# Prompt's selected and window attention: both heads' weights scaled on GpSimd, none on VectorE

## The reference, cut to what matters

```python
s = jnp.where(mask[:, :, None, None, :], s, NEG)
m = jnp.max(s, axis=-1, keepdims=True)
p = jnp.exp(s - m)
l = jnp.sum(p, axis=-1, keepdims=True)
o = jnp.einsum('bqgrk,bkgd->bqgrd', (p / l).astype(v.dtype), v)
...
o_nsa = (gate[:, :, 0, :, :, None] * o_cmp + gate[:, :, 1, :, :, None] * o_sel
         + gate[:, :, 2, :, :, None] * o_win)
```

## Time and profile before

| | |
|---|---|
| median of 3 runs | 2716.4 us (2714.63 to 2722.9) |
| the profiled execution's own time | 2721.63 us |
| its span, first to last instruction | 2718.8 us |
| TensorE busy over the span | 2513.0 us, 92% |
| VectorE, ScalarE, GpSimd busy | 1172.3, 934.7, 853.3 us |
| the stage `nsa_prompt` | about 471 to 634 us |

### The profile page before, as it was taken

How to read it: one execution, slowest core, us unless ns; L and a number is a source line. 1 busy time by engine, 2 the same in 40 slices (tenths; PEclk the granted TensorE clock), 3 DMA queues, 4 the chain that set the end, 5 groups by cost and what they waited for, 6 DMA issues and landing times. The chain is left out here.

```text
span 2718.8 us, 44972 instructions
## 1 busy us (share of the span) xinstructions
PE 2513.0 (92%) x18691; PEld 2248.3 (83%) x18691; DVE 1172.3 (43%) x2554; ACT 934.7 (34%) x1769; POOL 853.3 (31%) x434
## 2 busy tenths in 40 slices
PE   8889999997999999999988998899988888999997
PEld 8856796555989999998987897787765688999997
DVE  6884403776223222242754464441146424322225
ACT  4442221564332121133453464322135434221121
POOL 2350330332254333334333333323310026433331
PEclk9999998998999999999999899889998998999999
DMA  5212375450222222222221121113320822222221
GB/s 179 80 45 87 64 146 158 157 215 4 63 63 78 94 78 78 94 78 88 75 69 34 34 78 37 33 63 101 95 95 1 233 82 70 83 89 78 82 89 51
DMA packets 206728, 232.78 MB, mean 86 GB/s; under 512 B 40508, under 2 KB 165276, under 8 KB 205918
## 3 DMA queue, kind: packets, MB, share of 16 engines
q1 hardware_dynamic: 204446, 229.66, 27.3%
q10 hardware_dynamic: 2080, 0.25, 0.1%
HBM read 207.93 MB, written 48.35 MB: 94 GB/s over the span
## 5 line engine op out<-in xcount | busy, mean ns | idle before, releaser
L295 POOL TENSOR_TENSOR WRr<-WR,WH 128x2048 fp32r<-128x2048 f32 (+2 forms) x100 | 441.2, 4412 | 962.4 <-ACT WH L283 948.5
L2428 PE MATMUL PS<-HHr,WRr 128*128 128x288 f32 x1104 | 326.6, 296 | 0.0
L535 PE MATMUL PS<-YTr,WRr 128*128 128x288 f32 x1024 | 303.6, 297 | 0.0
L283 ACT CAST WH<-WR 128x2048 fp32r<-128x2048 f32 (+2 forms) x100 | 182.3, 1823 | 343.9 <-DMA WR<-in_mlp_w 141.6
L535 PE MATMUL PS<-HHr,WH 128*128 128x288 f32 (+1 forms) x896 | 271.4, 303 | 12.2 <-PEq L114 6.7
L535 PE MATMUL PS<-YTr,lt_WX 128*128 128x288 f32 x1408 | 282.1, 295 | 0.0
L535 PE MATMUL PS<-HHr,WRr 128*128 128x288 f32 (+1 forms) x896 | 268.3, 299 | 0.0
L535 PE MATMUL PS<-HTr,WH 128*128 128x288 f32 (+1 forms) x896 | 268.3, 299 | 0.0
L295 POOL TENSOR_TENSOR WRr<-WR,lt_WX 128x2048 fp32r<-128x2048 f32 x34 | 157.9, 4644 | 254.6 <-ACT lt_WX L283 254.6
L2428 PE MATMUL PS<-HHr,WH 128*128 128x288 f32 x800 | 236.8, 296 | 0.3 <-POOL WRr L295 0.3
L2428 PE MATMUL PS<-HTr,WH 128*128 128x288 f32 x800 | 236.2, 295 | 0.0
(11 more groups left out here) (685 smaller groups left out, 5680.2 us busy)
## 6 DMA issues: line engine op xcount, KB each, us to landing
WR<-in_mlp_w SPq DMA_DIRECT2D x64, 1024.0 KB, 5.2
WR<-in_cd_w_in SPq DMA_DIRECT2D x34, 1024.0 KB, 5.2
out_dil_s<-in_cache_dil_kv SPq DMA_DIRECT2D x2, 7936.0 KB
WR<-in_ab_w_in SPq DMA_DIRECT2D x12, 1024.0 KB, 5.2
past_rows<-in_cache_nsa_kv SPq DMA_DIRECT2D x16, 256.0 KB, 3.4
WR<-in_ab_w_in SPq DMA_DIRECT2D x16, 256.0 KB, 4.4
WR<-in_nsa_ck_w SPq DMA_DIRECT2D x4, 1024.0 KB, 5.4
WR<-in_nsa_cv_w SPq DMA_DIRECT2D x4, 1024.0 KB, 5.7
```

The costliest lines, as they stand in the source:

```text
L283: act.copy(high_slot(K, i, used), K.WR[:, n % RING, 0:used]).then_inc(K.hi, 1)
L295: pool.tensor_tensor(K.WRr[:, n % RING, 0:used], K.WR[:, n % RING, 0:used], high_slot(K, i, used).bitcast(F32), ALU.subtract).then_inc(K.l ...
L535: last = pe.matmul(out, a, b, start=(n == 0), stop=(n == 3 * len(terms) - 1))
L2428: last = pe.matmul(out, a[:, k, c], h[:, k, x], start=(n == 0), stop=(n == 3 * KT - 1))
```

## The change

GpSimd now scales both heads of a unit, one operation after the other, and VectorE none. `back(u)` on VectorE keeps the reciprocal alone. The two semaphores `p_even` and `p_odd` become one, `p_ready`, which both GpSimd operations raise; TensorE and ScalarE wait for it once in place of twice.

```diff
@@ turn(u), TensorE
-                    pe.wait_ge(p_even, u + 1)
-                    pe.wait_ge(p_odd, u + 1)
+                    pe.wait_ge(p_ready, 2 * (u + 1))
@@ exponentials, ScalarE
-                        act.wait_ge(p_even, u - 2)
-                        act.wait_ge(p_odd, u - 2)
+                        act.wait_ge(p_ready, 2 * (u - 2))
@@ GpSimd
-                    pool.tensor_scalar(E[:, u % 3, 0, 0:L], E[:, u % 3, 0, 0:L], sm[:, u % 3, 0:1], gate(u, 0),
-                                       ALU.mult, ALU.mult).then_inc(p_even, 1)
+                    for g in range(2):
+                        pool.tensor_scalar(E[:, u % 3, g, 0:L], E[:, u % 3, g, 0:L], sm[:, u % 3, g:g + 1], gate(u, g),
+                                           ALU.mult, ALU.mult).then_inc(p_ready, 1)
@@ back(u), VectorE
                     dve.reciprocal(sm[:, u % 3, :], sm[:, u % 3, :]).then_inc(r_ready, 1)
-                    dve.wait_ge(r_ready, u + 1)
-                    L = (units[u][1] + 1) * P
-                    dve.tensor_scalar(E[:, u % 3, 1, 0:L], E[:, u % 3, 1, 0:L], sm[:, u % 3, 1:2], gate(u, 1),
-                                      ALU.mult, ALU.mult).then_inc(p_odd, 1)
```

More of the change, by code:

```diff
@@ L1948, in nsa_prompt @@
         sm = sb("p_sm", [P, 3, 2])
-        with stage(nc, "s_mm", "nm_ready", "exp_done", "r_ready", "p_even", "p_odd", "turned", "t_act", "t_dve", "pv_done",
-                   "y_out", "zeroed", "gates_out", "dve_link") as (block, s_mm, nm_ready, exp_done, r_ready, p_even, p_odd, turned, t_act, t_dve,
+        with stage(nc, "s_mm", "nm_ready", "exp_done", "r_ready", "p_ready", "turned", "t_act", "t_dve", "pv_done",
+                   "y_out", "zeroed", "gates_out", "dve_link") as (block, s_mm, nm_ready, exp_done, r_ready, p_ready, turned, t_act, t_dve,
                                             pv_done, y_out, zeroed, gates_out, dve_link):
```

## The result

The changed kernel takes 2725.7 us (median of 20 runs, 2717.4 and up) against 2718.1 for the kernel before beside it. The ratio is 1.0023, with the 95% interval [1.0015, 1.0030]: 6.3 us slower. By the forecast's own basis, 2716.4 us, the ratio makes 2722.6. Either way it is above the forecast 2713.3 and outside its range. It is less than 0.3%, so among the chances it falls under "no change that can be told", but sign and size of the reasoning were wrong.

What follows compares the result with a forecast made beforehand. TensorE's own stream was taken as most of the stage, so only its waits could go. Gains of 1.8 + 0.9 + 0.6 = 3.3 us, less 0.2, gave net -3.1: 2716.4 becomes 2713.3 us, range 2709 to 2721.

Steps and rivals of the forecast that it cites:

- no change that can be told: For the whole kernel, a result within 0.3%, 8 us, of the kernel before; chance 0.9.
- What comes after the barrier has the same work and starts earlier by that: Behind the prompt's stage, later stages were to do the same work and pass on the stage's net -3.1 us.
- The scaling's price on GpSimd: One GpSimd scaling alone was to take about 0.29, 0.40, 0.50, 0.61 us for the four lengths, a pair 0.53 to 1.17.
- the rival without an exclusion: VectorE and GpSimd do not exclude each other; each GpSimd scaling costs 0.52 to 1.04 us again: +7 us, 2723.5; chance 0.12.
- the first rival: GpSimd's fixed part per scaling is at its upper bound, 0.41 us: +1.0 to +1.6 us in all, 2718; chance 0.2.
- the point at which I had the sign turn: In the prompt's stage, gain was to become loss where GpSimd's pair of 512-column scalings costs about 1.5 us.
- the sign of a wrong forecast: A pair of 512 columns over 1.5 us, or turns 20 to 22 waiting for GpSimd, would make the forecast wrong.
- The merged semaphore: One wait for two was to take 0.11 us off every turn (a unit's transposes) that waits for ScalarE's copy.
- VectorE's relief: Without its scaling, VectorE's output copy was to start 0.14 us behind the reciprocal, not 0.53, 0.39 us gained at turn 27.
- The period: The prompt's stage repeats every eight units; this was to take 19.5 to 19.6 us rather than 20.0, all the gain there.
- the tail at the barrier: At the stage's end GpSimd might be 0.13 us later at the barrier after its last pair; 0.2 us allowed.

Runs made afterwards that it cites:

- e2: The kernel before, with TensorE waiting for VectorE's scaling by name only in unit 0 (63 wait instructions fewer); ratio 1.0016 to the kernel before.
- e3: The changed kernel once more, unedited, for a second profile; ratio 1.0041 to the kernel before.
- e7: The changed kernel with head 1's weights left unscaled, so GpSimd scales once per unit; the prompt's stage takes 159.68 us, 163.51 in the changed kernel.
- e9: The kernel before with 192 more wait instructions on TensorE's list, for things past, in `scores`; ratio 1.0040 to the kernel before.
- e5: The changed kernel with a second wait on its one semaphore before each turn, restoring TensorE's list to 16741 instructions; ratio 0.9999 to the kernel before.
- e13: The changed kernel with 60 padding waits in `scores` for what is long past, TensorE's list at 16737 instructions; ratio 0.9988 to the kernel before.
- e10: The kernel before with one more VectorE memset of 1024 numbers at the end of the prompt's stage; ratio 1.0016 to the kernel before.
- e1: The changed kernel with the two semaphores `p_even` and `p_odd` kept apart, TensorE's list as long as before; ratio 1.0022 to the kernel before.
- e15: e1 once more, unedited, for a second profile; one run, the prompt's stage takes 165.23 us.
- e14: The kernel before with only the order of waits in `turn` changed, the two copies first, the weights' semaphores last; ratio 0.9996 to the kernel before.
- e11: The changed kernel with padding waits in `scores`, of which those for ScalarE's copy were not past; ratio 1.0145 to the kernel before.

## Why the prediction was wrong

- **"What comes after the barrier has the same work and starts earlier by that"** is the step that failed. The work is the same; the list is not. In the five profiles whose list is cut at that place (changed, e2, e3, e7, e9) C is 75.00 to 80.65, mean 77.7; in the twelve others 70.71 to 72.80, mean 72.2. So the cut costs 5.4 us on average, and with A's -1.1 makes +4.4 of the measured +6.3, [4.1, 8.2]. The forecast was -3.1. e5 and e13 take the cut away and leave no loss.
- The same sentence is unsafe at B, though this did not cost the changed kernel anything: 52.64 and 51.44 in its two profiles, 52.53 and 52.50 before. With the same work B took 45.4 to 61.3 us over the seventeen profiles, by whether VectorE's small operations meet GpSimd's long ones and by the clock (e10). It is most of e1's loss in e1's profile (5.1 us, A's 0.9 beside it) and less in e15's (1.8). That a later end of A can lengthen it is supported by e10's profile but not proven by its times: the interval of the whole begins at 1.1 us, and A alone gives 1.2. Which shifts do it is not shown.
- **The scaling's price on GpSimd** was mis-sized: 0.45, 0.56, 0.66, 0.77 us against 0.29 to 0.61. The slope is right (0.83 ns a column, forecast 0.82), and the rival without an exclusion is refuted: 768 ns alone where it had 1040. The fixed part is 0.34 us, not 0.19, between my value and the first rival's 0.41. A pair of 512 columns takes 1.52, just the point at which I had the sign turn. GpSimd thus became last at the turns, which I had named as the sign of a wrong forecast; GpSimd's busy time is 77.9 us and not 60. By e1 and e15, the change without the merged semaphore makes A 0.7 to 0.9 us longer. The first rival, at +1.0 to 1.6, is near that by luck: its sum had no cost of a wait instruction behind GpSimd's scaling, and with the merged semaphore A is 1.1 us shorter.
- **The merged semaphore** was right in kind and too small: 0.9 us forecast, 165.52 - 163.51 = 2.0 by e1, 1.6 by e5. The forecast let it work only behind ScalarE's copies, and in the changed kernel GpSimd releases the turns. e14 gets more out of the kernel before by order alone, 2.8 us.
- **VectorE's relief**: right. The y copy starts 0.07 us behind its reciprocal (521.20, 521.27) where it was 0.53, and the waits for its copies are gone.
- **The period** came out at 19.74 for 19.5 to 19.6, and not all of the stage's difference is in it: the tail at the barrier was mis-sized. The last copies ahead of the barrier, of the changed kernel and then of the one before, are below. GpSimd ends at 631.56 + 3.87 = 635.43, and TensorE's first load behind the barrier comes 0.85 us behind the y copy's end (634.20 + 0.69) where it came 0.29 behind it (634.65, 634.94). That is 0.56 for my 0.2. Seven or eight passes at 0.26 are 1.8 to 2.1 us, less 0.56, where A shows 1.1; the last 0.2 to 0.5 I did not place.

```profile
631.56 3.87 POOL L2072 COPY a_KV<-a_QT 64x64 f32<-64x64 f32 x16
...
634.20 0.69 DVE L2102 COPY YT<-PS 128x512 f32<-128x512 f32 x1 [1.28 <-PE PS L2024]
```

```profile
633.96 0.69 DVE L2107 COPY YT<-PS 128x512 f32<-128x512 f32 x1 [1.28 <-PE PS L2025]
```

## What to carry to other kernels

Count the instructions that an edit adds to or takes from an engine's list, and look in the trace after it for "issue" in the middle of a group of equal products: here such a stop belonged to the loading of the list, and some waits for things long past moved it. Such waits must really be past and off the path: 60 of them cost A nothing in e13, 192 cost 2.4 us in e9, and in e11 they cost 40. Judge an edit by its own stage first, from a profile, and by the whole afterwards; here a gain of 1 us and a loss of 5 were both real, and they lie 1.5 ms apart. Work moved to an engine that is almost last makes that one last at many turns; price it from the receiving engine's slope and a generous fixed part.

## What the runs showed of the hardware

- TensorE's list arrives in pieces of 256 instructions: 148 packets for 38051 instructions, stops behind loads 14531 and 14657 of the same kernel, and the same stop with 16677 and 16933 instructions. A piece that comes late stops TensorE for 3.4 to 3.7 us, with further stops of 0.6 to 1.6 in e3, e7 and e9. Why the transfer of the piece at this cut starts late, and not the cut 64 instructions earlier (0.42 us), stays open. The DMA engines are full there with the caches' transfers (q1 above), which was not varied. The Trainium skill, "Runtime: NRT & Kernel Launch", section "Instruction fetch mechanics", gives the same size of a block, 256 instructions, and calls the crossing of its edge mostly hidden; here it is not hidden at one place, as the 3.4 to 3.7 us show.
- GpSimd's scaling of 512 columns takes 768 ns alone and 1040 where VectorE's falls beside it; VectorE's takes 546 and, alone, 544. Where GpSimd's 4.5 us operation (L295) is already running, VectorE pays: a copy of 4 columns took 3.88 us for 0.17. The Trainium skill, "GPSIMD Engine Reference", section "Engine selection", calls one-input work on GpSimd roughly line-rate; 768 against 544 is 1.4 times as long, and 449 against 344 at 128 columns.
- Stage B took 45.4 to 61.3 us for the same work, with none, one or two of VectorE's small operations held for 3.7 us and more by GpSimd and a mean granted clock of 0.88 (e13) to 0.64 (e1).
